# Branch C's input projections moved from the head loop into seven-product quads

## What is computed

```python
h = _rmsnorm(x, norm_g[l])
proj = jnp.einsum('bsd,df->bsf', h, w_in[l])
parts = jnp.split(proj, SPLIT_POINTS, axis=-1)
aq, ak, av, az = parts[0:4]                 # branch A: differential attention, 8 heads
b_qkv = parts[4:4 + 3 * n_g]                # branch B: three groups of dilated attention
bz = parts[4 + 3 * n_g]
cb, cc, cx, cz = parts[5 + 3 * n_g:9 + 3 * n_g]
gates = jax.nn.sigmoid(parts[9 + 3 * n_g] + gate_b[l])
...
u = jnp.pad(cc * cx, ((0, 0), (C_CONV - 1, 0), (0, 0)))
conv = sum(conv_w[l][j] * u[:, j:j + seq] for j in range(C_CONV))
yc = cb * conv * jax.nn.silu(cz)
merged = gates0 * (ya @ w_branch_a) + gates1 * (yb @ w_branch_b) + gates2 * (yc @ w_branch_c)
x = x + jnp.einsum('bsd,de->bse', merged, w_out[l])
return _rmsnorm(x, final_g)
```

## Time and profile before

| | us |
|---|---|
| median of 3 runs | 2617.54 (2613.76 to 2617.56) |
| profiled execution, its time | 2612.32 |
| its span, first to last instruction | 2610.5 |
| PE busy / DVE busy / ACT busy | 2585.1 / 1698.8 / 935.7 |
| granted TensorE clock, mean | 0.998 of full speed |
| one head (from one head's values of branch B to the next's) | 215.24 |
| chain that ended last: PE / DVE / DMA / ACT | 94% / 3% / 1% / 1% |

### The profile page before, as it was taken

How to read it: one execution, slowest core, us unless ns; L and a number is a source line. 1 busy time by engine, 2 the same in 40 slices (tenths; PEclk the granted TensorE clock), 3 DMA queues, 4 the chain that set the end, 5 groups by cost and what they waited for, 6 DMA issues and landing times.

```text
span 2610.5 us, 31512 instructions
## 1 busy us (share of the span) xinstructions
PE 2585.1 (99%) x11886; PEld 2135.0 (82%) x11886; DVE 1698.8 (65%) x2053; ACT 935.7 (36%) x1182; POOL 0.2 (0%) x4
## 2 busy tenths in 40 slices
PE   9999999999999999999999999999999999999998
...
PEclk9999999999999999999999999999999999999999
DMA  5534453552543445355254332245544546787565
GB/s 190 172 131 136 148 188 98 185 192 85 193 160 116 135 170 166 101 182 188 93 190 157 122 97 89 86 158 188 178 161 141 190 162 193 267 289 243 208 225 194
DMA packets 121019, 428.63 MB, mean 164 GB/s; under 512 B 11313, under 2 KB 11570, under 8 KB 118962
## 3 DMA queue, kind: packets, MB, share of 16 engines
...
HBM read 361.54 MB, written 65.01 MB: 163 GB/s over the span
## 4 chain that ended last, share of the span: by engine, by line
PE 94%; DVE 3%; DMA 1%; ACT 1%; issue 1%; SPq 0%; DVEq 0%; ACTq 0%
PE proj L467 21%; PE proj L469 21%; PE proj L468 21%; PE tr_ps L467 3%; PE tr_ps L468 3%; PE tr_ps L469 3%; PE sc_ps L467 3%; PE sc_ps L468 3%; PE sc_ps L469 3%; PE o_ps L468 2%; PE o_ps L469 2%; PE o_ps L467 2%; PE tr_ps L508 2%; PE sc_ps L500 1%; DVE w_lo L1107 1%
## 5 line engine op out<-in xcount | busy, mean ns | idle before, releaser
L467 PE MATMUL proj<-act_hi,w_hi 128*128 128x512 f32 x2304 | 908.9, 394 | 0.5 <-DVE act_lo L1151 0.2
L469 PE MATMUL proj<-act_hi,w_lo 128*128 128x512 f32 x2304 | 899.1, 390 | 0.0
L468 PE MATMUL proj<-act_lo,w_hi 128*128 128x512 f32 x2304 | 898.0, 390 | 0.0
L754 ACT ACTIVATE w_hi<-raw 128x1024 fp32r<-128x1024 f32 x288 | 304.5, 1058 | 825.3 <-PE proj L469 820.5
L1103 DVE TENSOR_TENSOR w_lo<-raw,w_hi 128x1024 fp32r<-128x1024 f32 x288 | 352.6, 1224 | 374.4 <-ACT w_hi L754 373.0
L469 PEld LDWEIGHTS proj<-act_hi,w_lo 128*128 128x128 f32 x2304 | 432.7, 188 | 90.8
L467 PEld LDWEIGHTS proj<-act_hi,w_hi 128*128 128x128 f32 x2304 | 433.2, 188 | 89.3 <-issue 1.2
L468 PEld LDWEIGHTS proj<-act_lo,w_hi 128*128 128x128 f32 x2304 | 433.4, 188 | 86.1
L1107 DVE TENSOR_TENSOR w_lo<-raw,w_hi 128x1024 fp32r<-128x1024 f32 x188 | 229.6, 1223 | 106.7 <-ACT w_hi L758 106.1
L758 ACT ACTIVATE w_hi<-raw 128x1024 fp32r<-128x1024 f32 x188 | 199.3, 1061 | 244.9 <-PE tr_ps L469 69.5
L758 ACT ACTIVATE w_hi<-kb 128x1024 fp32r<-128x1024 f32 x120 | 127.3, 1061 | 183.9 <-PE proj L469 65.9
...
## 6 DMA issues: line engine op xcount, KB each, us to landing
...
ssum<-ws ACTq DMA_DIRECT2D x20, 2048.0 KB, 9.3
s_dram<-ssum ACTq DMA_DIRECT2D x20, 2048.0 KB, 7.5
...
kb<-wg SPq DMA_DIRECT2D x10, 2048.0 KB, 7.9
...
```

Of the source, the lines that this page charges most:

```text
L467: nc.tensor.matmul(out, w_h, a_h, start=first, stop=False, skip_group_check=shared)
L468: nc.tensor.matmul(out, w_h, a_l, start=False, stop=False, skip_group_check=shared)
L469: return nc.tensor.matmul(out, w_l, a_h, start=False, stop=last, skip_group_check=shared)
L754: nc.scalar.activation(w_hi[slot_w][:, :], raw[slot_raw][:, :], ACT.Copy).then_inc(hi_done, 1)
```

## The change

Branch C leaves the heads. A head has 14 blocks (28 units), with AZ and BZ last. Its columns of `w_in` (cc, cx, cz, cb, in this order) become quads 0 to 3 of what are now 10 quads before merging; the gates are quads 4 to 9. Their evictions take no bias, no tanh, and are stored to `c_dram`. Quad 0's weight sums are made in the heads (24 sets in all, four in each of heads 1 to 6, none in head 0) and come through the ring with its plain quarters, 28 units. Branch B's values and join of head i move behind block 0 of head i+1, those of head 7 into quad 0. `combine_h` works in blocks 1 to 7 of head 7. The loops on PE, ACT and DVE run twice over three written-out heads, since 28 is no multiple of the ring. From step 8 of quad 4 on, 20 steps for each head, `tail` loads the head's 128 columns of the four parts from `c_dram` (ACT queue, 256 KB each, pieces of 512 B) into two tiles in `rows`, makes the SiLU and cb times it, has PE turn both products to channels by tokens (`turn_tail`), and makes the taps from PSUM; the last of the 8 heads ends with step 27 of quad 9.

```diff
-NBLK1, NHU1 = 18, 36
+NBLK1, NHU1 = 14, 28
...
-AQ, AK, AV, AZ, Q0, K0, Q1, K1, Q2, K2, V0, V1, V2, BZ, CB, CC, CX, CZ = range(NBLK1)
+AQ, AK, AV, Q0, K0, Q1, K1, Q2, K2, V0, V1, V2, AZ, BZ = range(NBLK1)
 
 
 PRODUCTS, STEPS = 7, 28
-QUADS_G, QUADS_O = 6, 2
+QUADS_C, QUADS_G, QUADS_O = 4, 10, 2
 QUADS_B, STEPS_B, NU = 6, 14, 4
 R_G = W1
 R_B = R_G + QUADS_G * STEPS
 R_O = R_B + QUADS_B * STEPS_B
-X_B = 8 * QUADS_G
+X_K = STEPS
+X_B = X_K + 8 * (QUADS_G - 1)
 X_O = X_B + QUADS_B * STEPS_B
 I_O = 2 * QUADS_B
-SUMMED = I_O + NU * QUADS_O
+I_C = I_O + NU * QUADS_O
+SUMMED = I_C + NU
...
-LOAD_AT, SUM_AT = {1: 0, 4: 1, 9: 2}, {2: 0, 7: 1, 10: 2}
+LOAD_AT, SUM_AT = {0: 0, 3: 1, 6: 2, 9: 3}, {1: 0, 4: 1, 7: 2, 10: 3}
+TAIL, TAIL_STEP = STEPS * QUADS_C + 8, 20
...
-            sp.wait_ge(o_ready, 2 * HEADS)
-            sp.wait_ge(y_stored[0], 16 * (HEADS + 1))
-            for u in range(NU):
-                load_k1(0, u)
-            for q in range(QUADS_G):
+            for n in range(STEPS):
+                load_unit(n, I_C + n % NU, n // NU)
+                if n == 14:
+                    sp.wait_ge(o_free, 2 * HEADS + 1)
+                    sp.wait_ge(y_stored[0], 16 * (HEADS + 1))
+                    sp.dma_start(kb[:, 0:4096], wg[1, W22, :, :]).then_inc(k2_in, 16)
+                if n == 18:
+                    sp.dma_start(kb[:, 4096:8192], wg[1, W21, :, :]).then_inc(k3_in, 16)
+                if 20 <= n < 24:
+                    load_k1(1, n - 20)
...
+                    if w == 0:
+                        values_b(i - 1)
...
+            with pe.Fori(0, 2) as j:
+                for k in range(1, 4):
+                    blocks(looped(j, k))
+            blocks(fixed(HEADS - 1))
+
+            def turn_tail(h, at):
+
+                if at == 6:
+                    pe.wait_ge(c_v, h + 1)
+                    if h:
+                        pe.wait_ge(c_y, h)
+                    for n in range(4):
+                        end = nc.tensor.transpose(v_ps[:, P * n:P * (n + 1)], c_b[:, P * n:P * (n + 1)], ident[:, :])
+                    end.then_inc(c_vt, 1)
+                if at == 12:
+                    pe.wait_ge(c_u, h + 1)
+                    for n in range(4):
+                        end = nc.tensor.transpose(u_ps[:, P * n:P * (n + 1)], c_z[:, P * n:P * (n + 1)], ident[:, :])
+                    end.then_inc(c_ut, 1)
...
+            def between_g(q, p):
+
+                def after(u):
+                    if q == p == u == 0:
+                        values_b(HEADS - 1)
+                    h, at = divmod(STEPS * q + NU * p + u - TAIL, TAIL_STEP)
+                    if 0 <= h < HEADS:
+                        turn_tail(h, at)
+                return after
...
+            def load_head(h, n, tile):
+                act.dma_start(tile.rearrange("p (s q) -> p s q", s=4),
+                              c_dram[n, :, :, P * h:P * (h + 1)].rearrange("s p q -> p s q")).then_inc(c_in, 16)
+
+            def tail(h, at):
+
+                if at == 0:
+                    if h == 0:
+                        for n in range(8):
+                            act.wait_ge(g_stored[n], 16 * QUADS_C)
+                    act.wait_ge(y_stored[2], 16 * (h + 1))
+                    load_head(h, 2, c_z)
+                if at == 2:
+                    act.wait_ge(c_in, 64 * h + 16)
+                    nc.scalar.activation(c_b, c_z, ACT.Tanh, scale=0.5).then_inc(c_th, 1)
+                if at == 4:
+                    act.wait_ge(c_silu, h + 1)
+                    load_head(h, 3, c_b)
+                if at == 8:
+                    act.wait_ge(c_v, h + 1)
+                    load_head(h, 0, c_z)
+                if at == 10:
+                    act.wait_ge(c_vt, h + 1)
+                    load_head(h, 1, c_b)
+                if at == 18:
+                    act.wait_ge(c_y, h + 1)
+                    act.dma_start(y_dram[2 * HEADS + h, :, :], c_b).then_inc(y_stored[2], 16)
...
+                if q == 0:
+                    src = raw[(W1 + n) % RING][:, :]
...
-                    if w == CX:
-
-                        dve.wait_ge(evac_done, NBLK1 * i + (RING + CX + 1))
-                        link(tt(u[:, 2:T + 2], blk[CC][:, :], blk[CX][:, :], ALU.mult))
-                        link(ts(blk[CC][:, :], u[:, 2:T + 2], taps[:, 2:3], None, ALU.mult))
-                        link(stt(blk[CC][:, :], u[:, 1:T + 1], taps[:, 1:2], blk[CC][:, :], ALU.mult, ALU.add))
-                        link(stt(blk[CC][:, :], u[:, 0:T], taps[:, 0:1], blk[CC][:, :], ALU.mult, ALU.add))
-                        link(tt(blk[CC][:, :], blk[CC][:, :], blk[CB][:, :], ALU.mult))
-                    if w == CZ:
-                        silu(i, 2, CZ)
-                        dve.wait_ge(y_stored[2], 16 * i + 16)
-                        dve.wait_ge(y_stored[1], 16 * i + 32)
-                        stt(y_c[:, :], blk[CC][:, :], 0.5, blk[CZ][:, :], ALU.mult, ALU.mult).then_inc(y_ready, 1)
...
                     if first:
                         if q:
                             dve.wait_ge(g_stored[2 * d + s], 16 * q)
+                        if q < QUADS_C:
+                            ts(tile, bank[:, :], scale, None, ALU.mult).then_inc(got, 1)
+                            continue
...
+            def tail(h, at):
+
+                if at == 3:
+                    dve.wait_ge(c_th, h + 1)
+                    stt(c_z, c_b, 1.0, c_z, ALU.add, ALU.mult).then_inc(c_silu, 1)
+                if at == 6:
+                    dve.wait_ge(c_silu, h + 1)
+                    dve.wait_ge(c_in, 64 * h + 32)
+                    tt(c_b, c_b, c_z, ALU.mult).then_inc(c_v, 1)
+                if at == 12:
+                    dve.wait_ge(c_in, 64 * h + 64)
+                    tt(c_z, c_z, c_b, ALU.mult).then_inc(c_u, 1)
+                taps = [cols[:, S_CONV + 3 * h + n:S_CONV + 3 * h + n + 1] for n in range(3)]
+                if at == 15:
+                    dve.wait_ge(c_ut, h + 1)
+                    link(ts(c_b, u_ps[:, :], taps[2], None, ALU.mult))
+                if at == 16:
+                    for n in (1, 0):
+                        d = 2 - n
+                        link(stt(c_b[:, d:T], u_ps[:, 0:T - d], taps[n], c_b[:, d:T], ALU.mult, ALU.add))
+                if at == 17:
+                    dve.wait_ge(c_vt, h + 1)
+                    stt(c_b, c_b, 0.5, v_ps[:, :], ALU.mult, ALU.mult).then_inc(c_y, 1)
...
-                    if n < 4:
+                    if q and n < 4:
                         add_units(R3, q, n)
-                    if 4 <= n < 8:
+                    if q and 4 <= n < 8:
                         add_units(R2, q, n - 4)
-                    if 12 <= n < 16:
+                    if q and 12 <= n < 16:
...
+    w_quads = np.concatenate([w_in[:, (c0 + n * nb) * P:(c0 + (n + 1) * nb) * P] for n in (1, 2, 3, 0)] + [w_in[:, g0:]], axis=1)
```

More of the change, by code:

```diff
@@ L23 @@
 from contextlib import ExitStack
+from dataclasses import dataclass
 import concourse.bass as bass
@@ L80, with slot, bank, loads @@
 Y_AT = {0: [7, 9, 10, 11], 2: [9, 10, 11, 13]}
-LOAD_AT, SUM_AT = {1: 0, 4: 1, 9: 2}, {2: 0, 7: 1, 10: 2}
+LOAD_AT, SUM_AT = {0: 0, 3: 1, 6: 2, 9: 3}, {1: 0, 4: 1, 7: 2, 10: 3}
+TAIL, TAIL_STEP = STEPS * QUADS_C + 8, 20
 R1, R3, R2, R4 = range(4)
+@dataclass
+class Head:
+    i: object
+    k: int
+    j: object = None
+    def slot(self, t):
+        return (NHU1 * self.k + t) % RING
+    def bank(self, w):
+        return (NBLK1 * self.k + w) % RING
+    def loads(self, t):
+        n = (NHU1 * self.k + t) // RING + 1
+        return n if self.j is None else NHU1 * self.j + n
+def fixed(n):
+    return Head(n, n)
+def looped(j, k):
+    return Head(RING * j + k, k, j)
 def evicted(q, p, s):
     return 2 * PRODUCTS * q + 2 * p + s + 1
+def ring_12(q, u):
+    return X_K + 8 * (q - 1) + u
+def ring_22(q, u):
+    return ring_12(q, u) + NU
 def summed(kind, q, u):
-    return 16 * q + 4 * kind + u + 1
+    return 16 * (q - 1) + 4 * kind + u + 1
 def weights(p):
@@ L127, in program @@
     ALU, ACT, AX = mybir.AluOpType, mybir.ActivationFunctionType, mybir.AxisListType
+    c_dram = nc.dram_tensor("c_dram", (QUADS_C, T // P, P, D // 2), f32, kind="Internal").ap()
     y_dram = nc.dram_tensor("y_dram", (3 * HEADS, P, T), f32, kind="Internal").ap()
@@ L191, in program @@
             slope = s1("slope", [P, 4])
-            taps = s1("taps", [P, 3])
             nmax, sums, rsum = s1("nmax", [P, 2]), s1("sums", [P, 2]), s1("rsum", [P, 2])
-            blk = {b: stage[b % 2] for b in STAGED} | qk | {AZ: z, BZ: z, CZ: z, CB: cb, CC: cc, CX: cx}
+            blk = {b: stage[b % 2] for b in STAGED} | qk | {AZ: z_a, BZ: z_b}
             sq_a, inv_a = th, tmp_a
@@ L222, in program @@
             gin_r = s3("gin_r", [P, 4 * 1024], f32r)
+        pb = [ctx.enter_context(nc.psum_tensor(f"proj{i}", [P, T], f32)) for i in range(RING)]
+        sc_ps = [ctx.enter_context(nc.psum_tensor(f"sc_ps{i}", [P, T], f32)) for i in range(2)]
```

(16 more changed lines are left out.)

324 lines of the change are left out of this document (167 added, 157 removed).

## The result

| us | before | after | forecast |
|---|---|---|---|
| median of four runs | 2615.65 (2612.27 to 2617.56) | 2584.08 (2582.52 to 2584.22) | 2577 |
| profiled execution: time, span | 2612.3, 2610.5 | 2582.5, 2580.7 | 2572.5, 2571 |
| first of the gates' matmuls | 1735.50 | 1386.21 | |

The account below looks back on a forecast made before the run. PE, busy 2585.1 of 2610.5 us at full clock, was taken as the bound. Terms -43.5 + 7.0 - 8.8 + 1.5 + 3 + 1 = -39.8 us take the profiled 2612.3 to 2572.5, the median to 2577.5; range 2567 to 2600.

Parts of the forecast that it names:

- three signs of being wrong: ACT or DVE waiting over 2 us for head loads, then PE; quad 0 above 80 us; a head above 173 us.
- Term 1: Heads and first quads: 192 fewer matmuls, at 0.2267 us each, all on PE's path: -43.5 us.
- Term 2: Quads 4 to 9: 16 groups of four PE transposes for branch C, 0.44 us each: +7.0 us, bounds 5.6 to 9.6.
- Term 3: Quad 0: ready weight sums remove DVE's old stall, -8.8 us; DMA may be late next, +1.5 us.
- Term 4: Quads 4 to 9: branch C's elementwise work on DVE and waits for small head loads, +3 us, bounds 0 and 24.
- rival (b): Head loads mildly late, near 9.4 us, or colliding only beside 2 MB loads: 2590 to 2610 us, chance 0.12.
- DVE's crowding in quads 8 and 9: Branch C's operations in DVE's tightest stretch of quad 8, 2.7 us of backlog, just fit; last quad's second half fully booked.
- Term 5: Heads: DVE busy 108 of 171.7 us; a 2 us surplus at blocks 4 and 10 is worked off, no cost.
- Term 6: Start of the merged stage: DVE enters with the last head's operations behind it, loss of 2.4 us may become 3.4: +1.0.

Follow-up runs that it names:

- 5: Changed kernel with 192 matmuls put back in quads 1 to 3 (values change): those quads take 272.0 us, span 2632.9 us.
- 2: Changed kernel with experiment 1's edit, and the 2 MB kb loads of quads 1 to 8 each split into four of 512 KB: 2574.65 us, ratio 0.9853.
- 4: Changed kernel without branch C's 32 head loads, tiles holding 0.5, all engine work kept: 2576.70 us, span 2574.9.
- 1: Changed kernel with quad 0's kb loads issued as twelve of 512 KB, spread among ring units and begun sooner: 2582.11 us, ratio 0.9876.
- 6: Changed kernel without branch C's tail (no loads, tanh, convolution or transposes), a tile of 0.5 stored instead: 2567.83 us, span 2565.7.
- 7: Changed kernel with PE's head loop written out without a jump: 2582.84 us, span 2581.1; all six periods between heads 171.73 to 171.75 us.
- 8: Changed kernel with the edits of experiments 2 and 7 together: 2570.78 us, ratio 0.9834, span 2567.2.
- 3: Changed kernel with DVE's head loop written out without a branch: 2584.55 us, span 2582.8; the long head stays at 173.99 us.

## Why the prediction was right, and where 10 us went

The number held because the two large terms, the saved matmuls and quad 0's old stall, were right, and because the range reached 23 us above the likeliest value. The mechanism was right only in part. The prediction named three signs of being wrong, and all three appeared: ACT and DVE waited for head loads for up to 5.3 us with PE waiting for w_lo behind them, quad 0 took over 80 us with ACT waiting for raw (only 3.14 of its 7.7 extra us are branch B's values, which the forecast for quad 0 left out), and one head took 173.85 us. All errors went the same way, so none hid another.

| term | forecast | measured | shown by |
|---|---|---|---|
| 1 products | -43.5 | -43.5 | 5; heads of 171.75, quads of 76.16 |
| 2 transposes | +7.0 | +7.8 | quad 4; 2 and 4 |
| 3 quad 0 | -8.8 + 1.5 | -8.8 + 4.5 | 1 |
| 4 tail in quads 4 to 9 | +3 | +7.1 | 2, 4, 6 |
| 5 heads | 0 | +2.1 | 7, 8 |
| 6 merged stage and on | +1.0 | +1.1 (409.26 to 410.39) | one span; other runs 408.8 to 411.3 |
| sum | -39.8 | -29.7 | span: -29.8 |

**Term 1** held: on a bound engine that never rests, a matmul removed is worth its spacing (0.227), not its length (0.390).

**Term 2** was right in kind and 10% too low, since the spacing behind a group recovers over more matmuls than the row read for it showed. The Trainium skill ("TensorE: Matmul & The Clock Gate", Part 4: PE-mode transpose) has some 275 ns for a transpose in a kernel. The page's tile is bf16. For the float32 ones here the trace has 272 ns as the length of one, and 0.485 / 4 = 0.12 us as what one adds to PE's time. So the row decides, and that length must not be multiplied by the count. The prediction worked out, as an estimate at the page's 275 ns, a gain of 29 us in place of 40. That is close to the 29.8 measured only by chance: the transposes cost 7.8 us, not 17.6.

**Term 3** had the right successor, DMA in place of DVE, and the wrong measure. I compared bytes with the best rate over 33 us (34 against 33) and took 1.5. The bytes did fit: over these 33 us 341 GB/s moved at a share of 0.88, and 375 at 0.93 behind the second 2 MB load (the quad's mean, 256 at 0.71, hides this). What the sum of bytes left out is which transfer waits. The ring's units, one of which is wanted every 2.72 us, took up to 8.4 us in place of 4.3, while loads of kb that DVE reads only from step 24 on moved beside them. Experiment 1 moves the same bytes sooner and in smaller pieces and gets 3.5 of 4.5 us back.

**Term 4** is the step that failed most, by 4.1 us. The distribution was wrong: I took the median of the nearest row, 5.8, as the measure of the size, while nearly all of the loss is made by four loads behind a 2 MB one, all past the slack of 8.1 to 10.6 us that I had counted; a load of 7.3 us made ACT wait (2.9 us) and PE not. This was rival (b), "collide only beside the 2 MB loads". Its mechanism came true at a chance of 0.12; its time, some 20 us above the forecast, was too high, since only five of the 32 loads were waited for and they cost 6.6 us (experiment 4). The Trainium skill ("DMA: Bandwidth & Descriptors", Queues, rings and completion order) has the DMA engines go between queues by whole packets. The runs agree with it in direction: 11.4 to 12.7 us beside L471, at most 5.8 and 6.3 in experiments 2 and 8, where all is in pieces of 512 KB. But these also issue the pieces a step apart, so that size and pace are not told apart; the engines were 93 to 99% busy during the four late loads; and no run isolates the alternation itself. The other half of term 4, DVE's crowding in quads 8 and 9, cost at most 0.2 of the 0.5 us left in experiments 2 and 4.

**Term 5** named DVE's order in the heads as the risk and priced it at nothing, rightly: five of the six periods are at 171.75. The 2.1 us came from PE's own sequencer, which the prediction didn't look at: the jump became longer (4.97 us, not 3.3 to 3.9), and where the loop now ends six short transposes are part of what is queued to cover it.

**Term 6** is not confirmed by its 1.1: experiments 1 to 5, with the same tail and the same stages behind it, have 410.1 to 411.3, but experiments 7 and 8 have 408.8 and 409.0, no more than before's 409.26.

Left open: how much of the gains of experiments 1 and 2 is the pieces' size and how much their pace and earlier start, why the jump lasts 4.6 to 5.1 us in these kernels and 3.3 to 3.9 in before, and why the time to the first head's values lies anywhere from 192.4 to 197.4 us in the nine profiled executions with the change (PE then waits for xacc or x near 11 to 15 and 38 us).
